# Attention heads in pairs, weight roundings spread over the value panel, and branch merges ahead of the low halves

## The reference, cut to what matters

```
first block:   h = rms_norm(x);  qa, ka, va, qb, kb, vb, ga, gb, mg = split(h @ w_in)
  ya = banded_attention(qa, ka, va, 128, bias, sink) * silu(ga)     8 heads of 64, 2 key/value heads
  for g, (window, dilation) in enumerate(((128,1), (512,4), (2048,16))):
      outs[g], lses[g] = dilated_group(qb[g], kb[g], vb[g], ...)    8 heads of 64 each
  yb = sum(softmax(lses) * outs) * silu(gb)
  merged = sigmoid(mg0 + b0) * (ya @ w_branch_a) + sigmoid(mg1 + b1) * (yb @ w_branch_b)
  x = x + merged @ w_out
layer, twice:  z = rms_norm(x) @ w_in
  o_nsa  = gates of (compressed keys, all keys, window)             8 query heads, 2 key/value groups
  o_ret  = layer_norm(decayed q k^T v) * silu(g)                    4 heads
  o_conv = silu(layer_norm(conv31(a * sigmoid(b))))
  merged = sum over 3 branches of sigmoid(mg_i) * (o_i @ w_branch_i)
  x = x + merged @ w_out
  x = x + relu(rms_norm(x) @ w_ff1)**2 @ w_ff2
result: rms_norm(x)
```

## Time and profile before

| | |
|---|---|
| median of 3 runs | 1280.48 us (1279.82 to 1283.36) |
| profiled execution | 1283.56 us |
| its span in the trace | 1281.8 us |
| granted TensorE clock, mean of the span | 0.981 |
| TensorE busy | 1228.7 us, 96% |
| VectorE busy | 849.9 us, 66% |
| ScalarE busy | 548.8 us, 43% |
| low parts of the weights (L562, VectorE) | 185 of 2256 ns, 415.3 us |
| roundings of the weights (L537, ScalarE) | 185 of 1888 ns, 348.2 us |
| DMA | 206.54 MB, 161 GB/s over the span |

### The profile page before, as it was taken

How to read it: one execution, slowest core, us unless ns; L and a number is a source line. 1 busy time by engine, 2 the same in 40 slices (tenths; PEclk the granted TensorE clock), 3 DMA queues, 4 the chain that set the end, 5 groups by cost and what they waited for, 6 DMA issues and landing times.

```text
span 1281.8 us, 17250 instructions
## 1 busy us (share of the span) xinstructions
PE 1228.7 (96%) x6920; PEld 1044.1 (81%) x6920; DVE 849.9 (66%) x1315; ACT 548.8 (43%) x687; POOL 35.3 (3%) x43
## 2 busy tenths in 40 slices
PE   7999999999999899999999999999899998999996
PEld 5788778787898677777899888997776876999885
DVE  4566455447779878867576644598989676677542
ACT  5555454344434533443344433434434533534431
POOL 1121000000000000000000000000000000000000
PEclk9999999799999899999999999999999999999998
DMA  8457634236445423344455655545323444455540
GB/s 292 169 167 251 209 123 137 89 109 242 168 161 179 156 82 117 131 139 160 162 177 185 213 191 184 190 141 196 127 99 102 162 163 146 152 196 171 209 164 33
DMA packets 39467, 206.54 MB, mean 161 GB/s; under 512 B 4003, under 2 KB 13731, under 8 KB 16307
## 3 DMA queue, kind: packets, MB, share of 16 engines
q1 hardware_dynamic: 39052, 205.22, 46.8%
q10 hardware_dynamic: 336, 0.22, 0.1%
HBM read 204.23 MB, written 1.20 MB: 160 GB/s over the span
## 4 chain that ended last, share of the span: by engine, by line
PE 84%; DVE 9%; DVEq 3%; ACT 2%; issue 1%; DMA 0%; POOL 0%; POOLq 0%; ACTq 0%
PE panel L841 17%; PE panel L843 16%; PE panel L842 16%; PE panel L864 7%; PE panel L863 7%; PE panel L862 7%; PE tile L892 4%; DVE ring_parts L562 3%; DVE area L1942 2%; PE heads_out L1043 2%; DVEq L1943 1%; PE tile L988 1%; PE panel L880 1%; PE tile L1176 1%; PE tile L950 1%
## 5 line engine op out<-in xcount | busy, mean ns | idle before, releaser
L562 DVE TENSOR_TENSOR ring_parts<-ring,ring_parts 128x2048 fp32r<-128x2048 f32 (+1 forms) x185 | 415.3, 2256 | 160.9 <-ACT ring_parts L537 142.8
L537 ACT ACTIVATE ring_parts<-ring 128x2048 fp32r<-128x2048 f32 (+1 forms) x185 | 348.2, 1888 | 255.6 <-PE panel L843 199.4
L841 PE MATMUL panel<-ring_parts,hT_high 128*128 128x512 f32 (+2 forms) x688 | 285.4, 415 | 2.8 <-DVE hT_low L1664 1.2
L843 PE MATMUL panel<-ring_parts,hT_low 128*128 128x512 f32 (+2 forms) x688 | 268.4, 390 | 0.0
L842 PE MATMUL panel<-ring_parts,hT_high 128*128 128x512 f32 (+2 forms) x688 | 267.4, 389 | 0.0
L862 PE MATMUL panel<-hT_high,ring_parts 128*128 128x256 f32 x704 | 199.4, 283 | 0.0
L864 PE MATMUL panel<-hT_high,ring_parts 128*128 128x256 f32 x704 | 199.2, 283 | 0.0
L863 PE MATMUL panel<-hT_low,ring_parts 128*128 128x256 f32 x704 | 199.2, 283 | 0.0
L841 PEld LDWEIGHTS panel<-ring_parts,hT_high 128*128 128x128 f32 x688 | 131.6, 191 | 44.8 <-issue 22.9
L841 PE MATMUL panel<-ring_parts,area_parts 128*128 128x512 f32 x384 | 152.2, 396 | 4.5 <-DVE tok L1813 4.5
L843 PEld LDWEIGHTS panel<-ring_parts,hT_low 128*128 128x128 f32 x688 | 131.4, 191 | 27.7
(11 more groups left out here) (227 smaller groups left out, 1164.8 us busy)
## 6 DMA issues: line engine op xcount, KB each, us to landing
ring<-in_w_layers_dram SPq DMA_DIRECT2D x140, 1024.0 KB, 4.9
ring<-in_w_first_dram SPq DMA_DIRECT2D x40, 1024.0 KB, 5.1
area<-bias_rows SPq DMA_DIRECT2D x16, 160.0 KB, 3.0
ring<-in_w_layers_dram SPq DMA_DIRECT2D x4, 560.0 KB, 3.9
area<-bias_rows SPq DMA_DIRECT2D x16, 96.0 KB, 3.0
area<-bias_rows SPq DMA_DIRECT2D x1, 1536.0 KB, 8.7
area<-in_gains_dram SPq DMA_DIRECT2D x3, 512.0 KB, 5.8
x<-in_x_dram SPq DMA_DIRECT2D x2, 512.0 KB, 4.8
```

The costliest lines, as they stand in the source:

```text
L537: act.activation(ring_lo[:, SLOTS + hi, 0:w], ring[:, slot, 0:w], ACT.Copy).then_inc(high_ready, 1)
L562: g.tensor_tensor(ring_lo[:, slot, 0:w], ring[:, slot, 0:w], ring_lo[:, SLOTS + hi, 0:w], ALU.subtract).then_inc(low_ready, 1)
L841: pe.matmul(ps[:, b, 0:width], high, hi[:, k, :], start=first, stop=False)
L843: mm = pe.matmul(ps[:, b, 0:width], low, hi[:, k, :], start=False, stop=last)
```

## The change

1. **Pairs.** The units of A and of a layer go in the order 0, 4, 1, 5, 2, 6, 3, 7; B keeps 0 to 7. Two neighbours make a pair, whose operands lie on different rows of the array. The scores of a pair are one step, its matmuls written in turns, one of the one head, one of the other, each head into its own PSUM tile. The steps go S of pair 0, then T, T, S of the next pair (two steps for B: g 0 and g 1), V, V, and in a layer an empty step behind these. ScalarE's exponential runs two units ahead. Outputs are gathered and scattered by the new order (`place_of`, `heads_of_group`).
2. **Value panel.** One by one instead of by twos: ScalarE rounds w1v at the end of qkr, vr/1 at vr 1, mg0/0 at vr 4 and mg0/1 at vr 6; VectorE makes the low parts of w1v at vr 0, vr/1 at vr 2, mg0/0 at vr 5 and mg0/1 at vr 7.
3. **Merge.** The low parts stand behind each merge, not ahead of it, and the three instructions of the third branch move behind the merge of branch 0.
4. **Output.** The second chunk of merged sums is transposed behind k-step 2 of wo0. The low part named by wo0/1 is made ahead of `operand_parts`. ff0 waits for each weight half at its first use, not for both at its start.

The core of the diff:

```diff
+PAIRS = [0, 4, 1, 5, 2, 6, 3, 7]
...
-    return [("A", h, 1) for h in range(H)] + [("B", h, 2) for h in range(H)]
+    return [("A", h, 1) for h in PAIRS] + [("B", h, 2) for h in range(H)]
 def units_layer():
-    return [("s", h, 1) for h in range(H)] + [("w", h, 1) for h in range(H)]
+    return [("s", h, 1) for h in PAIRS] + [("w", h, 1) for h in PAIRS]
...
-def unit_steps(n):
-    out = [("S", 0)]
-    for u in range(n):
-        if u + 1 < n:
-            out.append(("S", u + 1))
-        out += [("T", u), ("V", u)]
+def pair_steps(units, spare):
+    def scores(p):
+        return [("S", p, g) for g in range(units[2 * p][2])]
+    pairs = len(units) // 2
+    out = scores(0)
+    for p in range(pairs):
+        out += [("T", 2 * p), ("T", 2 * p + 1)]
+        if p + 1 < pairs:
+            out += scores(p + 1)
+        out += [("V", 2 * p), ("V", 2 * p + 1)] + [None] * spare
     return out
...
-FIRST_PLAN = make_plan(FIRST_WIDE, unit_steps(2 * H), range(KC), {("mg2", 3): ["yA"]})
-LAYER_PLAN = make_plan(LAYER_WIDE, unit_steps(2 * H), (0, 1, 2, 3, 4, 5, 7), {
+FIRST_PLAN = make_plan(FIRST_WIDE, pair_steps(units_first(), 0), range(KC), {("mg2", 3): ["yA"]})
+LAYER_PLAN = make_plan(LAYER_WIDE, pair_steps(units_layer(), 1), (0, 1, 2, 3, 4, 5, 7), {
...
+        for e, u, *g in steps:
+            if e == "S":
+                out += [score_tile(units[2 * u + i], g[0]) for i in range(2)]
+            elif e == "T":
+                out += [f"T{units[u][0]}{units[u][1]}{g}" for g in range(units[u][2])]
...
+        def place_of(kind, u):
+            u = u % GROUP
+            u = u if kind == "B" else 2 * (u % 2) + u // 2
+            return slice(u * HD, (u + 1) * HD)
+        def heads_of_group(t, i):
+            return t.rearrange("p (s n) -> p s n", s=2)[:, :, 2 * HD * (i % 2):2 * HD * (i % 2 + 1)]
...
-                parts_of = [[w.rearrange("p (k n) -> p k n", k=KC) for w in wait_parts(part, f"{name}/{i}")] for i in range(2)]
                 for group in range(2):
                     if group:
                         before_last()
                     for i in range(2):
-                        hi, lo = parts_of[i]
+                        hi, lo = (w.rearrange("p (k n) -> p k n", k=KC) for w in wait_parts(part, f"{name}/{i}"))
...
-                         after={1: lambda: turn_columns(part, "m", tok, 1, merged, base)})
+                         after={2: lambda: turn_columns(part, "m", tok, 1, merged, base)})
...
+            def scores_first(p, g):
+                pair = units[2 * p:2 * p + 2]
+                outs = [tile_for(part, score_tile(unit, g)) for unit in pair]
+                mm = [None, None]
+                for b in range(NB):
+                    bs, to = slice(b * P, (b + 1) * P), slice(b * TOKENS, (b + 1) * TOKENS)
+                    if pair[0][0] == "A":
+                        for i, (_, h, _) in enumerate(pair):
+                            r, c = head_rows(h)
+                            mm[i] = pe.matmul(outs[i][0][:, to], qaT[r, c, bs], kaT[r, :], start=True, stop=True)
+                    elif g == 0:
+                        for i, (_, h, _) in enumerate(pair):
+                            r, c = slice(HD * (h % 2), HD * (h % 2) + HD), h // 2
+                            mm[i] = pe.matmul(outs[i][0][:, to], qbT[r, 0, c, bs], kbT[r, 0, c, :], start=True, stop=True)
+                    else:
+                        for j, group in enumerate((2, 1)):
+                            s = b * TOKENS + j * P
+                            for i, (_, h, _) in enumerate(pair):
+                                r, c = slice(HD * (h % 2), HD * (h % 2) + HD), h // 2
+                                mm[i] = pe.matmul(outs[i][0][:, s:s + P], qbT[r, group, c, bs], kbT[r, group, c, bs], start=True, stop=True)
+                for i in range(2):
+                    mm[i].then_inc(outs[i][1], 1)
...
+                        pair = units[2 * u:2 * u + 2]
+                        w = 0 if pair[0][0] == "s" else 1
+                        outs = [tile_for(part, score_tile(unit, 0)) for unit in pair]
+                        for i, (_, h, _) in enumerate(pair):
+                            r, c = head_rows(h)
+                            pe.matmul(outs[i][0][:, 0:P], qT[r, c, 0:P], kT[r, w, 0:P], start=True, stop=True)
+                        for i, (_, h, _) in enumerate(pair):
+                            r, c = head_rows(h)
+                            pe.matmul(outs[i][0][:, P:3 * P], qT[r, c, P:TOKENS], kT[r, w, :], start=True, stop=True)\
+                              .then_inc(outs[i][1], 1)
...
+                        if u == 0:
+                            exp_layer(0)
+                            exp_layer(1)
...
-                    elif e == "V" and u + 1 < len(units):
-                        exp_layer(u + 1)
+                    elif e == "V" and u + 2 < len(units):
+                        exp_layer(u + 2)
...
-                        if s == 4:
-                            round_after(act, part, *(["vr/0", "w1v"] if p == "vr" else [f"{p}/0"]))
-                        for e, u in LAYER_PLAN[p, s]:
-                            step_layer(e, u)
+                        if s == 1 and p == "vr":
+                            round_after(act, part, "w1k")
+                        elif s == 4:
+                            round_after(act, part, f"{p}/0")
+                        elif s == 6 and p == "vr":
+                            round_after(act, part, "w1v")
+                        for e in LAYER_PLAN[p, s]:
+                            step_layer(*e)
                     if p == "qkr":
-                        round_after(act, part, "qkr/1", "w1k")
+                        round_after(act, part, "qkr/1")
...
+                if g == 0:
+                    v.wait_ge(E_loaded[load % 2], 64 * (load // 2 + 1) if kind == "A" else 32 * (load // 2 + 3))
+                    if u >= 2:
+                        k2, h2, n2 = units[u - 2]
+                        for g2 in range(n2):
+                            tile_of(v, part, f"T{k2}{h2}{g2}")
+                ps = tile_of(v, part, score_tile(units[u], g))
+                for b in range(NB):
+                    init = first[:, 12 + h:13 + h] if kind == "A" else low
+                    if g == 0:
+                        at = backwards(P * (1 - b), TOKENS, end=TOEP * (1 + (u % 2 if kind == "A" else 0)))
+                    else:
+                        at = backwards(0, TOKENS, end=5 * P)
+                    e = v.tensor_tensor_reduce(L[:, b, g * TOKENS:(g + 1) * TOKENS], ps[:, b * TOKENS:(b + 1) * TOKENS],
+                                               Es[:, load % 2, at], 1.0, init, ALU.add, ALU.max, mx[:, b, g:g + 1])
+                e.then_inc(tile_sem(part, score_tile(units[u], g)), 1)
+                if g < n - 1:
+                    return
...
-                        if i or c:
-                            lows_to(part, f"br{i if c else i - 1}{1 - c}/0")
...
-                lows_to(part, f"br{branches - 1}1/0")
+                        lows_to(part, f"br{i}{c}/0")
+                    if i == 0 and last_branch:
+                        last_branch()
...
-                before_wide = ["vsg/1", "w1k", "vr/1", *[f"{p}/1" for p in LAYER_WIDE[2:]]]
+                lows_at = {(p, 2): f"{q}/1" for p, q in zip(LAYER_WIDE, ["vsg"] + LAYER_WIDE)}
+                lows_at.update({(p, 6): f"{p}/0" for p in LAYER_WIDE})
+                lows_at.update({("vr", 0): "qkr/1", ("vr", 2): "w1k", ("vr", 5): "vr/0", ("vr", 7): "w1v"})
+                del lows_at["vr", 6]
                 for i, p in enumerate(LAYER_WIDE):
                     for s in range(KC):
-                        if s == 2:
-                            lows_to(part, before_wide[i])
-                        elif s == 6:
-                            lows_to(part, "w1v" if p == "vr" else f"{p}/0")
-                        for e, u in LAYER_PLAN[p, s]:
-                            step_layer(e, u)
+                        if (p, s) in lows_at:
+                            lows_to(part, lows_at[p, s])
+                        for e in LAYER_PLAN[p, s]:
+                            step_layer(*e)
...
-                v.wait_ge(conv_z, l + 1)
-                v.scalar_tensor_tensor(two("z"), two("tz"), 1.0, two("z"), ALU.add, ALU.mult)
-                v.drain()
-                hi, lo = parts(AREA_2["brT"], 2048, 1024), parts(LOW_OF_BRANCH[2], 0, 1024)
-                v.tensor_copy(hi, two("z"))
-                v.drain()
-                v.tensor_tensor(lo, two("z"), hi, ALU.subtract).then_inc(branch_ready, 1)
-                merge(part, 3, two("mgt").rearrange("p (i b n) -> p i b n", i=6, b=2), l * 4 + 4)
+                def conv_branch():
+                    v.wait_ge(conv_z, l + 1)
+                    v.scalar_tensor_tensor(two("z"), two("tz"), 1.0, two("z"), ALU.add, ALU.mult)
+                    v.drain()
```

(7 more changed lines are left out.)

175 lines of the change are left out of this document (79 added, 96 removed).

## The result

The changed kernel took 1244.69 us, the median of 4 runs (1241.45 to 1247.10), against 1280.15 for the kernel before (4 runs, 1279.08 to 1283.36): a ratio of 0.9714, 95% interval 0.9691 to 0.9737, 35.5 us or 2.8% faster. The forecast was 1236.8 in 1217 to 1258. The profiled execution took 1244.34 with a span of 1242.5, so 39.3 less span than the earlier trace rows's execution.

The account below looks back on a forecast made before the run. TensorE was taken as the path nearly everywhere, VectorE deciding up to mg0. Gains of 18.7 (first block), 3.9 (layers) and 21.1 (merge, output, ff0) sum to 43.7 us, taking the 1280.48 median to 1236.8 us, range 1217 to 1258.

Parts of the forecast that it names:

- Side by side: Attention score steps: two heads on rows 0-63 and 64-127 cost at best what one head costs; the best was taken.
- Rivals 1: Attention pairs run one after the other instead of side by side: 20 us less gain, 1257 us; chance 0.12.
- Rival 2: Attention pairs run side by side but in program order: 5 us, giving 1242 us; chance 0.05.
- First block: First block's attention: fewer score steps, paired B steps, a wait and its clock loss gone, less new waits; gain 18.7 us.
- new waits I named: First block's attention: first transposes 1.5 us late, T12 behind mg1 0.3, T15 needing a tile T14 holds 1.1.
- The clock's 6.8: First block's attention: the 6.8 us lost to the lowered clock behind the 2.98 wait goes.
- Merge, output, ff0: Block ends: waits and clock falls at br10, merged sums and ff0 go; 9.7 us per layer, 1.7 first block, 21.1 in all.
- Layers up to mg0: Layers, qkr to mg0: VectorE's queue sets the time; no gain in layer 1, layer 2 1.6 us behind the old time.
- one fall in each layer: Layers, at the 3.7 us TensorE wait at mg0: one clock fall costing 2.5 us, between 1.7 and 3.4.
- rival 3: New waits also pull the clock down, at T0 and S2 in each layer, T15 and V12: 11 us, 1248; chance 0.20.
- VectorE decides: Layers up to mg0: VectorE's queue holds the same work, its low half of mg0/0 ending about 444.4 in layer 1.
- Layers, mg0 to mg5: TensorE decides again: 4.4 us saved per layer; after clock and queue terms, 3.6 in layer 1, 0.3 in layer 2.

Follow-up runs that it names:

- the five with the same work up to mg0: Changed kernel with one head after the other (1246.14 us), two roundings later (1239.53), ff0 awaiting both halves (1247.93), third branch ahead of merges (1247.47), the last try (1247.90).
- the logits first: Changed kernel with one low part (qkr/1) moved from ahead of a layer's first logits to behind them; 1245.08 us.
- the last try: Changed kernel with ScalarE's two roundings later and the next two low parts made inside VectorE's gaps waiting for GpSimd; 1247.90 us.

## Why the prediction was right, and where it was wrong

**Side by side.** Right. One row of two meeting instructions, 10 ns apart, carried it, and the run on shared rows measured it: 0.86 for a pair in a layer (my 0.85 plus little), 1.07 for A. Rivals 1 and 2 are out. Rival 2 also by experiment, for pairs of up to four matmuls a head. (A slip in the sum: eight B steps of 2.1 are 16.8, not 16.6.)

**First block.** 19.3 and 2.0 against 18.7 and 1.7, of which 9.5 by the order and 9.7 by the rows. Of the new waits I named, T0 came with 1.30 (1.5), T12 with 0.43 (0.3), T15 did not come (1.1). The clock's 6.8 behind the old wait of the earlier trace rows is back in full.

**Merge, output, ff0.** 20.3 in the layers against 19.4, and it belongs to these edits alone. Two attributions inside were off. I gave ff0's gain to the order and the split wait together; the order does nearly all. I put 1.7 of clock on the third branch's wait; undone, the wait of 2.25 came back without it.

**Layers up to mg0: the step that failed.** I put VectorE's low half of mg0/0 at 45.9 behind the start of qkr; it ended at 47.6 (425.0) in layer 1 and at 47.9 in layer 2. The waits themselves I had nearly to the tenth; TensorE's in layer 1:

```profile
383.39 0.74 PE L933 MATMUL tile<-ident,area 128*128 128x128 f32 x3 [2.01 <-ACT area L1546]
...
405.21 0.49 PE L1227 MATMUL tile<-area 64*128 64x128 f32 x4 [1.25 <-DVE area L2199]
411.67 0.50 PE L883 MATMUL panel<-ring_parts,hT_high 128*128 128x512 f32 x1 [1.45 <-DVE ring_parts L576]
421.27 0.52 PE L933 MATMUL tile<-ident,area 128*128 128x128 f32 x3 [1.60 <-DVE area L2085]
425.14 0.77 PE L883 MATMUL panel<-ring_parts,hT_high 128*128 128x512 f32 x1 [3.35 <-DVE ring_parts L576]
```

Forecast: 2.1, 1.4, 1.4, 1.4, 3.7. What failed is the clock behind the first of them. I placed one fall in each layer, at mg0, and none at T0; that was left to rival 3. The changed kernel and the five with the same work up to mg0 have the wait of 2.0 at T0 in all of their twelve layers, with a fall behind it in seven and none in five. With the fall, qkr to mg0 took 47.8 in layer 1 and 48.0 to 48.1 in layer 2; without it 46.2 and 46.5, and the low half ended at 46.1 in layer 1. That is the forecast of 46.1 and, in layer 2, of 1.6 above the old 44.8. (The old stretches of the two layers differ by 1.2; for a queue that is equal in both I should have written 1.2 and not 1.6.) So the fall is worth 1.5 to 1.6 per layer, which is the whole miss of these two rows.

One execution shows both cases, that of the kernel with two roundings later: layer 1 (first line of each two) without the fall, layer 2 with it. TensorE's wait at T0, windows of its clock behind, VectorE at w1v's low half:

```profile
382.86 0.55 PE L933 MATMUL tile<-ident,area 128*128 128x128 f32 x3 [2.01 <-ACT area L1546]
839.60 0.90 PE L933 MATMUL tile<-ident,area 128*128 128x128 f32 x3 [2.01 <-ACT area L1546]
...
383.00:386.50 3.50, 3.50 (x20) 2.66 (x19) 3.42 (x5) 1.60 (x6) 0.00 (x0) 1.00 0.02 5
839.50:843.00 3.50, 3.40 (x10) 2.71 (x11) 3.42 (x5) 1.47 (x6) 0.00 (x0) 0.51 0.00 0
...
398.86 2.29 DVE L576 TENSOR_TENSOR ring_parts<-ring,ring_parts 128x2048 fp32r<-128x2048 f32 x1 [2.28 <-ACT ring_parts L551]
857.13 2.29 DVE L576 TENSOR_TENSOR ring_parts<-ring,ring_parts 128x2048 fp32r<-128x2048 f32 x1 [3.66 <-ACT ring_parts L551]
```

The last two lines show how a delay of TensorE reaches VectorE, which I had taken to run through by itself. The rounding of w1v follows ScalarE's copy of the key compression's result. That copy starts 21.0 behind the start of qkr in the changed kernel, 19.5 here in layer 1, and 18.1 with the logits first. VectorE comes to w1v's low half at 20.3, 19.7 and 20.5, and then stands 3.26, 2.28 and not at all. I had allowed 2.9 for its idle time in the whole stretch. In the term "VectorE decides", the engine that decides is fed by the one that waits for it.

**Layers, mg0 to mg5.** Forecast 3.6 and 1.9, measured 2.4 and 0.4. I had T12 and V12 with 1.8; the waits are 1.07, 0.49, 1.90 and 1.70, in all 5.2 (5.1 in layer 2). Two errors the other way hid half of that: the clock took 1.4 and 1.8 here where I had put 2.5, and with waits and clock taken out the stretch is 5.3 and 5.4 shorter where I had 4.4. That is luck. The terms I missed are one gap of VectorE and one order of ScalarE:

```profile
473.82 0.36 DVE L2173 TENSOR_SCALAR stat<-stat 128x4 f32<-128x4 f32 x2 [2.26 <-POOL stat L2341]
...
484.74 0.47 PE L883 MATMUL panel<-ring_parts,hT_high 128*128 128x512 f32 x1 [1.07 <-DVE ring_parts L576]
```

VectorE waits for GpSimd's root behind mg1 (2.26), which was there before, when no wait of TensorE stood at mg3; filled with a low half in the last try, it no longer cost the 1.07 there. And with exponentials two units ahead, ScalarE's roundings at the panel ends fall between the two exponentials of a pair; moving them gave 1.8 per layer.

**The clock.** I expected one fall of 2.5 in each layer. There were two in each: 1.7 at T0 in both, 1.7 and 3.4 around mg0. T0 is rival 3's place, though only one of the places that rival 3 asked for, and the falls there come and go between executions of the same code. By kind, the forecast was 28.3 of work and waits (measured 27.3) and 15.4 of clock (12.0): most of the 4.4 missing is clock. TensorE's busy time fell by 39.3 where I wrote some 25: I had left the clock out of that number, and slow matmuls count as busy.

## What to carry to other kernels

Two matmuls on different halves of the rows cost one if they are written near each other, so pair whatever uses 64 rows; look for a single place in the trace where two such instructions already meet before believing or doubting it. When a path has two engines that feed each other, a wait added to one is a gap in the other's queue some steps later: carry each delay around the loop once before calling one engine the bound. Before giving a fall of the clock to an edit, look at the same stretch in other traces whose code there is the same. Before a transfer or a rounding that nobody needs soon, ask what short step stands behind it in the engine's order; moving two of them was the cheapest gain here.
